# The first projection, the rotation tables and their place in the load queue

## The chip, the cores and the metric

The kernel runs on one core of one Trainium2 chip. Its engines are PE (TensorE, the matmul engine), DVE (VectorE), ACT (ScalarE), POOL (GpSimd) and SP (SyncE, which here only issues loads). They run their own instruction lists in order and wait for each other on semaphores. The metric is the device time of one execution in microseconds; less is better.

## The reference, cut to what matters

Two transformer-like blocks are computed on 256 tokens of width 1024. Only the front of the first one is touched here:

```
cs  = silu(c);  mod = cs @ mod_w[0] + mod_b[0]        # 1024 -> 6144: shift, scale, gate ...
h   = modulate(rms_norm(x, norm_g[0,0]), sh1, sc1)
proj = h @ ab_w_in                                     # 1024 -> 2048: u, q, k, v of 512 each
ab  = exp(lam * dt)                                    # complex, 32 groups x 64 states
x_t = ab * x_(t-1) + (b @ u_t);  y_t = Re(c @ x_t) + d_skip * u_t
y_ssm = gelu(y) * sigmoid(gelu(y) @ glu_w + glu_b)
y_att = attention of 8 heads of 64 with a bias per distance
x  += g1 * (concat(y_ssm, y_att) @ ab_w_out)
```

All data are float32.

## The kernel before, in words

**Weights and splits.** A stream of weight chunks, 128 x 2048 floats (1 MB) each, is loaded by SP into three buffers `raw[0..2]` (`load`, L573). ACT copies a chunk to `w_hi` in the type fp32r (`hi`, L745, the copy L751), DVE computes `w_lo = raw - w_hi` (`lo`, L1335, L1339). A product is then three fp32r matmuls, hi*hi, hi*lo and lo*hi (`three`, L2232). The activations are split in the same way into `h_hi` and `h_lo`. A `raw` buffer is free for the next chunk as soon as both halves have been made, long before PE uses them.

**The front.** PE computes the first 2048 modulation values from 16 pieces of 512 KB (`pm_piece`, L2183, four matmuls a piece, one for each 32 columns of the array), of which eight are in flight: six in `arena` and two in `raw[2]`. ACT takes the sums off (`pm_copy`, L881), PE turns them to columns (L2190), DVE adds the bias and makes the gains (L1493, L1524). x is normalized by DVE (L1517), turned by PE (`x_turn`, L2106), modulated by ACT (`x_upper`, L793, L795) and split by DVE (`x_lower`, L1540, L1541). The first chunk of `ab_in` is asked for behind twelve pieces.

**The projection `ab_in`** has 8 chunks of 16 products each (8 slices of the inner size, 2 output halves). Behind chunk c stand on PE `bu(c+1)` (input of state tile c+1, L2287) and, from c = 2, `y_of(c-2)` (output of a state tile, L2300). ACT copies a chunk out of PSUM (L905) and makes `w_hi` of chunk c+3; DVE makes `w_lo` of chunk c+3 and then runs `ssm_tile(c)` (L1611): multiply by the rotation table (L1615, L1616), add (L1618, L1619), scan (L1621), rotate back (L1630, L1632).

**The rotation tables** `e_re`, `e_im` hold cos and sin of angle * t for 16 tiles and 256 steps. They are outer products of two tables of 16 entries, made two tiles at a time by `e_pair` (L491, six operations L497 to L502): four pairs on DVE, four on POOL.

**The eight heads** follow. For head h, DVE runs `ssm_tile(8+h)`, `recip(h-1)` (L1667), `head(h)` (bias and maximum, L1658, L1661) and `turned_back(8+h)` (L1641, L1642). ACT scales the probabilities of head h-1 (`probs`, L913), takes the exponential of head h (L933), copies the turned probabilities of h-1 (L919) and last the output of h-1 (`head_copy`, L924). PE runs `bu`, `y_of`, the turn of head h-1 (L2106), up to five more modulation pieces, `head_out(h-1)` (L2352) and `scores(h+1)` (L2332). `y_out(n)` (L1647, DVE) adds the skip term to four finished tiles. Then come gelu (L944), the gate (`glu`, one chunk) and `ab_out` (four chunks).

Of the kernel before, what the change touches and what calls it, by code (L numbers as in the profile page):

```python
# [25 lines left out]
P = 128  # L26
T = 256
# [12 lines left out]
UT = SSM_G * SSM_H // P  # L40
HEADS, HD = 8, 64
# [33 lines left out]
CM_GROUPS = (2, 0, 3, 1)  # L75

# [179 lines left out]
def build(nc, A, out):  # L256
    with ExitStack() as ctx:
# [56 lines left out]
        e_re, e_im = at(E_TABLE, ST, T), at(E_TABLE + ST * T, ST, T)  # L314
# [4 lines left out]
        e1, e2 = (at(PREP + 512 * i, 2, ST, 16) for i in range(2))  # L319
        e_part = [at(a, 2, 16, 16) for a in (PREP + 1024, ARENA - 512)]  # L320
# [10 lines left out]
        pm_w = [at(a, PM_COLS) for a in (0, 1024, 2048, 3072, E_TABLE + 1024, E_TABLE + ST * T + 1024)]  # L331
        pm_w += [raw[2][:, i * PM_COLS:(i + 1) * PM_COLS] for i in range(2)]
        pm_late = [raw[i // 2][:, i % 2 * PM_COLS:(i % 2 + 1) * PM_COLS] for i in range(PM_LATE)]
        c_raw = hf[:, 0:4, :].rearrange("p (e a) (b c) -> p e (a b) c", e=2, c=32)
        c_tmp = [hf[:, 4 + 2 * i:6 + 2 * i, :].rearrange("p a (b c) -> p (a b) c", c=32) for i in range(2)]
# [153 lines left out]
        E_POOL = ST // 4  # L489

        def e_pair(v, link, g):  # L491

            j = slice(2 * g, 2 * g + 2)
            a, b = ([e[:, i, j, :].unsqueeze(k).broadcast_to([P, 2, 16, 16]) for i in range(2)] for e, k in ((e1, 3), (e2, 2)))
            er, ei = (t[:, j, :].rearrange("p j (a b) -> p j a b", b=16) for t in (e_re, e_im))
            part = e_part[g >= E_POOL]
            v.tensor_tensor(er, a[0], b[0], ALU.mult)  # L497
            link(v.tensor_tensor(part, a[1], b[1], ALU.mult))
            link(v.tensor_tensor(er, er, part, ALU.subtract))
            v.tensor_tensor(ei, a[0], b[1], ALU.mult)  # L500
            link(v.tensor_tensor(part, a[1], b[0], ALU.mult))
            return v.tensor_tensor(ei, ei, part, ALU.add)  # L502
# [49 lines left out]
        for n, v in enumerate(NORMS):  # L552
            pairs = v["kt"] // 2
            SQ.append(SQ[-1] + (0 if n in TOKEN or n == LAYER_NORM else pairs))
            UPPER.append(UPPER[-1] + (0 if n in (FINAL, FINAL_2) else DT // 2 if n in TURNED else 2 * pairs))
            SCALES.append(SCALES[-1] + (0 if n in TOKEN or n == LAYER_NORM else pairs))
            H.append(H[-1] + (pairs if n not in (FINAL, FINAL_2) else 0))

# [13 lines left out]
        def _(sp):  # L572
            def load(q, i=None):  # L573
# [60 lines left out]
            for m in range(PM_FIRST):  # L634
                load_pm(m)
                if m == 11:
                    load_plain("ab_in", 0, 1)
            load_plain("ab_in", 1, 2)
            sp.wait_ge(sem("pm_used"), PM_FIRST)
            load_plain("ab_in", 2, 6)  # L640
            sp.wait_ge(sem("h_ready"), H[1])
# [5 lines left out]
            sp.wait_ge(hi_done, Q["ab_out"] + 2)  # L647
            sp.wait_ge(lo_done, Q["ab_out"] + 2)
# [93 lines left out]
        def _(act):  # L742
            nxt = [0]

            def hi(q, i=None):  # L745
# [3 lines left out]
                if q >= SLOTS:  # L749
                    act.wait_ge(chunk_done, q - SLOTS + 1 + (0 if i is None else 6 * i))  # L750
# [33 lines left out]
            def x_upper(n):  # L784

                v, i = NORMS[n], TURNED.index(n)
                if n == 0:
                    act.wait_ge(sem("gates_known"), 1)
# [75 lines left out]
            act.dma_start(c_raw, A["ssm_c"].rearrange("p (e j c) -> p e j c", e=2, j=ST)).then_inc(sem("c_landed"), 16)  # L864
            act.dma_start(b_turned, A["ssm_b"].rearrange("p (e t s) -> p e t s", e=2, t=UT)).then_inc(sem("b_landed"), 16)
# [23 lines left out]
            hi_upto(0)  # L889
            pm_copy(1)  # L890
            x_upper(0)
            hi_upto(2)

            for c in range(8):
# [432 lines left out]
        def _(dve):  # L1327
# [92 lines left out]
            nc.vector.tensor_tensor(n0, abi, lr, ALU.mult)  # L1420
            link(nc.vector.tensor_tensor(n1, abr, li, ALU.mult))
            link(nc.vector.tensor_tensor(ci, n0, n1, ALU.subtract))
            link(nc.vector.tensor_tensor(ci, ci, den, ALU.mult))

            final_g = par[:, COL["final_g"]:COL["final_g"] + DT]
            nc.vector.tensor_tensor(both_g[:], final_g, par[:, COL["norm_mix_g_2"]:COL["norm_mix_g_2"] + DT], ALU.mult)
            link(nc.vector.tensor_tensor(both_q, final_g, final_g, ALU.mult))
            nc.vector.tensor_scalar(both_q, both_q, EPS, None, ALU.add).then_inc(sem("both_sum"), 1)
            dve.wait_ge(sem("c_landed"), 16)
# [1360 lines left out]
```

## Time and profile before

| | |
|---|---|
| median of 3 runs | 1525.33 us |
| lowest, highest | 1524.75, 1529.95 us |
| profiled execution, span from first to last instruction | 1526.8 us |
| PE, PEld, DVE, ACT, POOL busy | 94%, 78%, 74%, 51%, 3% |
| mean granted TensorE clock | 0.979 of full |
| chunk 0 of `ab_in` done (its copy L905 starts) | 64.84 us |
| chunk 7 done | 127.88 us |
| last head copied out | 200.84 us |

No time of the profiled execution is given beside its span; the span is 1.5 us above the median of the runs. An fp32 matmul stands in the profile as two instructions, an fp32r matmul as one. A row of the timeline gives a start in us, a duration in us, the engine, line, operation, tiles and shapes, and in brackets how long the engine had been idle and what ended that. A row of the chain gives start, duration and what it was.

### The profile page before, as it was taken

The numbers are of one execution on the slowest core, as the hardware profiler recorded it, in microseconds if no ns is written. First come the engines' busy times: TensorE is split into PE (matmuls) and PEld (weight loads), VectorE is DVE, ScalarE is ACT, GpSimd is POOL, SyncE is SP. The second block draws the span as 40 slices with busy tenths as digits, with TensorE's granted clock in tenths as the row PEclk, the third lists the DMA queues.
The fourth block names the chain that finished last, engine by engine and source line by source line (L and its number), as shares of the span: only waits on it lengthen the run. The fifth ranks groups of instructions, "written<-read, shape, count | busy, mean of one in ns | idle before, by whom it ended". The sixth has DMA issues, their size and how long they took to land.

```text
span 1526.8 us, 24920 instructions
## 1 busy us (share of the span) xinstructions
PE 1429.8 (94%) x9483; PEld 1193.0 (78%) x9483; DVE 1128.1 (74%) x1680; ACT 772.9 (51%) x1090; POOL 51.5 (3%) x38
## 2 busy tenths in 40 slices
PE   5498989999999999999999889999999999999998
PEld 1385568899976668999979655799997877799997
DVE  7999746988884457999984476686667858776666
ACT  3322356555563365555554666564546542455554
POOL 2600200000000000000001000000000000000000
PEclk9898999999999999999999999999999999999999
DMA  9332945988869766988734401355545433345551
GB/s 359 134 129 90 347 162 197 354 318 306 313 242 390 303 230 252 353 342 334 287 147 138 125 0 48 115 186 192 192 170 191 162 111 138 111 169 189 185 196 59
DMA packets 58060, 315.65 MB, mean 207 GB/s; under 512 B 7011, under 2 KB 8524, under 8 KB 33856
## 3 DMA queue, kind: packets, MB, share of 16 engines
q1 hardware_dynamic: 53826, 303.30, 53.8%
q10 hardware_dynamic: 4158, 11.30, 2.3%
q8 instruction: 52, 0.85, 0.2%
q14 instruction: 24, 0.20, 0.0%
HBM read 311.85 MB, written 1.15 MB: 205 GB/s over the span
## 4 chain that ended last, share of the span: by engine, by line
PE 75%; DVE 13%; ACT 5%; issue 4%; DMA 2%; ACTq 0%; SPq 0%; DVEq 0%; POOL 0%
PE bank L2232 62%; DVE w_lo L1339 2%; PE bank L2491 2%; ACT w_hi L751 1%; PE bank L2575 1%; PE bank L2106 1%; PE bank L2124 1%; PE bank L2183 1%; DMA arena<-in_mod_later 1%; PE bank L2300 1%; ACT hf L1256 1%; DVE h_lo L1541 1%; DVE hf L1553 1%; ACT hf L793 1%; DVE hf L1993 1%
## 5 line engine op out<-in xcount | busy, mean ns | idle before, releaser
L1339 DVE TENSOR_TENSOR w_lo<-raw,w_hi 128x2048 fp32r<-128x2048 f32 x186 | 426.2, 2292 | 169.6 <-ACT w_hi L751 168.4
L2232 PE MATMUL bank<-h_hi,w_hi 128*128 128x256 f32 x1800 | 517.3, 287 | 11.3 <-DVE h_lo L1541 9.7
L2232 PE MATMUL bank<-h_lo,w_hi 128*128 128x256 f32 x1800 | 510.8, 284 | 0.0
L2232 PE MATMUL bank<-h_hi,w_lo 128*128 128x256 f32 x1800 | 510.7, 284 | 0.0
L751 ACT ACTIVATE w_hi<-raw 128x2048 fp32r<-128x2048 f32 x186 | 355.8, 1915 | 129.8 <-PE bank L2232 114.6
L2232 PEld LDWEIGHTS bank<-h_hi,w_hi 128*128 128x128 f32 x1800 | 347.1, 193 | 21.3 <-DVE h_lo L1541 11.9
L2232 PEld LDWEIGHTS bank<-h_lo,w_hi 128*128 128x128 f32 x1800 | 347.0, 193 | 2.3 <-issue 0.7
L2232 PEld LDWEIGHTS bank<-h_hi,w_lo 128*128 128x128 f32 x1800 | 346.7, 193 | 0.0
L1756 DVE SCALAR_TENSOR_TENSOR arena<-bank,par,arena 128x255 f32<-128x255 f32 (+1 forms) x264 | 109.1, 475 | 111.5 <-ACT arena L988 79.1
L2232 PE MATMUL bank<-w_hi,a_hi 128*128 128x512 f32 x368 | 145.8, 396 | 4.9 <-DVE a_lo L1781 4.0
L2232 PE MATMUL bank<-w_hi,a_lo 128*128 128x512 f32 x368 | 144.3, 392 | 0.0
L2232 PE MATMUL bank<-w_lo,a_hi 128*128 128x512 f32 x368 | 144.1, 391 | 0.0
L988 ACT ACTIVATE arena<-bank,par 128x256 f32<-128x256 f32 x88 | 44.9, 560 | 139.4 <-PE bank L2232 139.4
L1367 DVE SCALAR_TENSOR_TENSOR arena<-arena,silu_c 128x384 f32<-128x384 f32 (+1 forms) x192 | 104.2, 611 | 0.0
L2232 PE MATMUL bank<-w_hi,h_hi 128*128 128x512 f32 (+1 forms) x224 | 86.5, 386 | 5.8 <-DVE hf L1553 3.0
L2232 PEld LDWEIGHTS bank<-w_hi,a_hi 128*128 128x128 f32 x368 | 69.6, 189 | 22.1 <-DVE w_lo L1339 5.0
L2232 PE MATMUL bank<-w_hi,h_lo 128*128 128x512 f32 (+1 forms) x224 | 84.8, 378 | 0.0
L2232 PE MATMUL bank<-w_lo,h_hi 128*128 128x512 f32 (+1 forms) x224 | 84.7, 378 | 0.0
L2232 PEld LDWEIGHTS bank<-w_lo,a_hi 128*128 128x128 f32 x368 | 69.5, 189 | 15.0
L2232 PEld LDWEIGHTS bank<-w_hi,a_lo 128*128 128x128 f32 x368 | 69.6, 189 | 13.0
L1006 ACT ACTIVATE a_hi<-arena 128x512 fp32r<-128x512 f32 x44 | 27.8, 632 | 61.9 <-DVE arena L1777 61.8
L2232 PEld LDWEIGHTS bank<-w_hi,h_hi 128*128 128x128 f32 x224 | 42.9, 191 | 18.4 <-issue 10.7
(327 smaller groups left out, 1703.5 us busy)
## 6 DMA issues: line engine op xcount, KB each, us to landing
raw<-in_stream SPq DMA_DIRECT2D x186, 1024.0 KB, 5.0
arena<-in_mod_stream SPq DMA_DIRECT2D x64, 768.0 KB, 7.5
arena<-in_mod_later SPq DMA_DIRECT2D x48, 512.0 KB, 8.0
raw<-in_mod_pe SPq DMA_DIRECT2D x36, 512.0 KB, 6.6
arena<-in_mod_pe SPq DMA_DIRECT2D x12, 512.0 KB, 12.7
sq<-row_store ACTq DMA_DIRECT2D x7, 512.0 KB, 3.5
sq<-in_bias SPq DMA_DIRECT2D x8, 256.0 KB, 6.7
x<-in_x_t ACTq DMA_DIRECT2D x1, 1024.0 KB, 8.6
```

The lines of the kernel that those rows point to most:

```text
L751: nc.scalar.activation(w_hi[s][:], raw[s][:], ACT.Copy).then_inc(hi_done, 1)
L793: nc.scalar.activation(hf[:, k, :], turned(n, k), ACT.Identity, **by).then_inc(sem("full_ready"), 1)
L988: ins = nc.scalar.activation(gate_c[:, e, :], half(4, e), ACT.Identity, scale=par[:, bass.ds(wb[center] + 2 * s + e, 1)], bias=par[:, bass ...
L1006: nc.scalar.activation(slot_hi(q), act_f, ACT.Copy)\
L1256: nc.scalar.activation(mla_s(h, t), bank[u % 4][:], ACT.Exp, bias=small[:, k + 1:k + 2], scale=MLA_SCALE, accum_out=small[:, k + 2:k + 3]) ...
L1339: nc.vector.tensor_tensor(w_lo[s][:], raw[s][:], w_hi[s][:].bitcast(F32), ALU.subtract).then_inc(lo_done, 1)
L1367: ins = nc.vector.scalar_tensor_tensor(parts[e], buf[:, kt % 4, :], silu_c[:, c0 + kt:c0 + kt + 1], parts[e], ALU.mult, ALU.add)
L1541: ins = nc.vector.tensor_tensor(v["parts"][1][:, k, :], hf[:, k, :], up.bitcast(F32), ALU.subtract)
L1553: ins = nc.vector.tensor_tensor(part, acc[:], row_at(gate_rows[gate], fh), ALU.mult)
L1756: ins = nc.vector.scalar_tensor_tensor(o, src, par[:, bass.ds(w[tap] + 2 * s + e, 1)], o, ALU.mult, ALU.add)
L2232: ins = nc.tensor.matmul(out_, l, r, start=first and n == 0, stop=last and n == 2, **kw)
L2491: ins = nc.tensor.matmul(bank[2 * part + ft][:], dft[:, part, t, ft * P:(ft + 1) * P], sources[part][:, t, 512 * s_:512 * s_ + 512], start ...
```

## The change

1. The eight `ab_in` chunks are not split (PLAIN = 8). PE multiplies `raw` by the unsplit `hf` in fp32 (`plain_chunk`), 16 matmuls a chunk in place of 48. The hi/lo counters start at chunk 8. A `raw` buffer is now free when PE has finished the chunk in it (`chunk_done`), up to chunk 10.
2. The normalized input is modulated once, four slices by ACT and four by DVE, with no `h_hi`, `h_lo`.
3. The tables are doubled instead: DVE makes 64 steps of all tiles in six rounds, and the steps to 128 and to 256 come tile by tile, each from two ACT copies with a scale (`twist`) and one DVE operation (`double`). POOL makes no tables.
4. The skip term is a PE matmul with a diagonal (`skip_diag`) that opens the sum of four tiles; `y_out` becomes an ACT copy.
5. Loads: the pieces use four buffers in `arena` and four in `raw[1]`, `raw[2]`; the first `ab_in` chunk is asked for behind all sixteen pieces; `ssm_b` and `ssm_c` move from ACT's queue at the start to SP's queue behind it; `x_turn(0)` stands behind piece 12 instead of 15; x is scaled before the tables are made, and the C matrix is prepared after the modulation.

```
-                if q >= SLOTS:
-                    sp.wait_ge(hi_done, q - SLOTS + 1 + more)
-                    sp.wait_ge(lo_done, q - SLOTS + 1 + more)
+                if q >= SLOTS + PLAIN:
+                    sp.wait_ge(hi_done, q - SLOTS + 1 - PLAIN + more)
+                    sp.wait_ge(lo_done, q - SLOTS + 1 - PLAIN + more)
+                elif q >= SLOTS:
+                    sp.wait_ge(chunk_done, q - SLOTS + 1)
...
-                if m == 11:
+                if m == 15:
                     load_plain("ab_in", 0, 1)
+            sp.dma_start(b_turned, A["ssm_b"]...)
+            sp.wait_ge(sem("pm_used"), 14)
             load_plain("ab_in", 1, 2)
+            sp.dma_start(c_raw, A["ssm_c"]...)
             sp.wait_ge(sem("pm_used"), PM_FIRST)
             load_plain("ab_in", 2, 6)
...
+            def twist(j, m):                                          # ACT
+                i = doubling(j, m)
+                if i == 1:
+                    act.wait_ge(sem("doubled"), 1)
+                if m == 2 * BASE:
+                    act.wait_ge(sem("doubled"), 1 + doubling(j, BASE))
+                k = m // BASE - 1
+                nc.scalar.activation(turns_[:, j, 0, m:2 * m], turns_[:, j, 1, 0:m], ACT.Copy, scale=pow_neg[:, k, j:j + 1])
+                nc.scalar.activation(turns_[:, j, 1, m:2 * m], turns_[:, j, 0, 0:m], ACT.Copy, scale=pows[6 + k][:, 1, j:j + 1])\
+                    .then_inc(sem("twisted"), 1)
...
             for c in range(8):                                        # ACT
                 nc.scalar.activation(dst, src, ACT.Copy).then_inc(bank_free, 1)
                 hi_upto(q + 3)
+                twist(c + 4, BASE)
+                twist(c + 2, 2 * BASE)
+                if c == 6:
+                    y_out(0)
...
             for h in range(HEADS):                                    # ACT
+                if h < 4:
+                    twist(12 + h, BASE)
+                if h < 6:
+                    twist(10 + h, 2 * BASE)
...
+            def double(j, m):                                         # DVE
+                k = m // BASE - 1
+                dve.wait_ge(sem("twisted"), doubling(j, m))
+                nc.vector.scalar_tensor_tensor(turns_[:, j, :, m:2 * m], turns_[:, j, :, 0:m], pows[6 + k][:, 0, j:j + 1],
+                                               turns_[:, j, :, m:2 * m], ALU.mult, ALU.add).then_inc(sem("doubled"), 1)
...
             for c in range(8):                                        # DVE
                 lo_upto(Q["ab_in"] + c + 3)
+                double(c + 4, BASE)
                 ssm_tile(c)
-                if c in (2, 4):
-                    link(e_pair(nc.vector, link, 1 + c // 2))
+                double(c + 2, 2 * BASE)
             for h in range(HEADS):
-                if h % 2 == 0:
-                    dve.wait_ge(sem("e_ready"), h // 2 + 1)
+                if h < 4:
+                    double(12 + h, BASE)
                 ssm_tile(8 + h)
+                if h < 6:
+                    double(10 + h, 2 * BASE)
...
+            def plain_chunk(c, q, fill):                              # PE
+                w = raw[q % SLOTS]
+                pe.wait_ge(raw_landed[q % SLOTS], LANDED[q])
...
+                    ins = nc.tensor.matmul(half(4 + fill % 2, n), *sides, start=c > 0 and k == 0, stop=k == DT - 1, skip_group_check=c == 0)
+                ins.then_inc(chunk_done, 1)
```

ACT, from the output copy of head 0 (L924 before, L944 now) to that of head 1. L913/L933 scale, L933/L961 exponentiate, L919/L939 copy the turned probabilities, L881/L872 is `pm_copy`. Before:

```order
L924 ACTIVATE arena<-bank 64x256
L913 ACTIVATE hf<-hf,small 128x256 x2
L933 ACTIVATE hf,small<-hf,small 128x256 x2
L919 ACTIVATE hf<-bank 128x512
L881 ACTIVATE arena<-bank 128x256
L924 ACTIVATE arena<-bank 64x256
```

Now:

```order
L944 ACTIVATE arena<-bank 64x256
L884 ACTIVATE arena<-arena 128x64
L885 ACTIVATE arena<-arena 128x64
L884 ACTIVATE arena<-arena 128x128
L885 ACTIVATE arena<-arena 128x128
L933 ACTIVATE hf<-hf,small 128x256 x2
L961 ACTIVATE hf,small<-hf,small 128x256 x2
L939 ACTIVATE hf<-bank 128x512
L872 ACTIVATE arena<-bank 128x256
L944 ACTIVATE arena<-bank 64x256
```

The first two of the four copies between them are `twist(14, 64)`, the other two `twist(12, 128)`.

DVE, from `turned_back(9)` (L1682, L1683) on, over tile 10 (L1656 to L1671), `recip(1)` (L1702) and `head(2)` (L1693, L1696), with the two `double` operations (L1625). Before, the same operations have the lines L1641 and L1642, L1615 to L1630, L1667 and L1658:

```order
L1641 TENSOR_TENSOR arena<-arena 128x256
L1642 TENSOR_TENSOR arena<-arena 128x256
L1615 TENSOR_TENSOR arena<-bank,arena 128x512
L1616 TENSOR_TENSOR arena<-bank,arena 128x512
L1618 TENSOR_TENSOR arena<-arena 128x256
L1619 TENSOR_TENSOR arena<-arena 128x256
L1621 SCALAR_TENSOR_TENSOR arena<-cols,arena 128x256 x2
L1630 TENSOR_TENSOR arena<-arena 128x512
L1667 RECIPROCAL small<-small 128x2
L1658 SCALAR_TENSOR_TENSOR hf<-bank,sq 128x512
```

Now:

```order
L1682 TENSOR_TENSOR arena<-arena 128x256
L1683 TENSOR_TENSOR arena<-arena 128x256
L1625 SCALAR_TENSOR_TENSOR arena<-arena 128x2x64
L1656 TENSOR_TENSOR arena<-bank,arena 128x512
L1657 TENSOR_TENSOR arena<-bank,arena 128x512
L1659 TENSOR_TENSOR arena<-arena 128x256
L1660 TENSOR_TENSOR arena<-arena 128x256
L1662 SCALAR_TENSOR_TENSOR arena<-cols,arena 128x256 x2
L1671 TENSOR_TENSOR arena<-arena 128x512
L1625 SCALAR_TENSOR_TENSOR arena<-arena 128x2x128
L1702 RECIPROCAL small<-small 128x2
L1693 SCALAR_TENSOR_TENSOR hf<-bank,sq 128x512
```

Added are `double(14, 64)` ahead of tile 10 and `double(12, 128)` behind it, each of which waits for its `twist`.

## Rows read from the trace of the kernel before

**Rows 1.** PE timeline, last modulation piece and x_turn (start us, us, what)
```profile
34.30 1.04 PE L2183 MATMUL bank<-raw,arena 128*32 128x256 f32 x8 [0.20 <-DMA raw<-in_mod_pe]
...
35.27 1.97 PE L2106 MATMUL bank<-ident_sb,hf 128*128 128x128 f32 x16
```

**Rows 2.** Windows (us; PE, PEld, DVE, ACT, POOL busy; PEclk; DMA share, GB/s)
```profile
6.00:33.00 27.00, 16.09 (x116) 3.78 (x116) 22.74 (x104) 10.86 (x23) 3.25 (x3) 1.00 1.02 412
...
76.00:80.00 4.00, 4.00 (x20) 3.86 (x20) 3.93 (x5) 0.00 (x0) 0.00 (x0) 0.57 0.48 203
...
144.00:154.00 10.00, 7.68 (x49) 3.34 (x50) 9.73 (x19) 2.83 (x9) 2.28 (x2) 0.52 0.33 115
```

**Rows 3.** DVE groups from 29.7 to 64 us (count, busy us, mean ns)
```profile
L1541 DVE TENSOR_TENSOR h_lo<-hf,h_hi 128x256 fp32r<-128x256 f32 x8 | 10.3, 1322 | 0.1
```

**Rows 4.** DVE groups from 64 to 135 us, same columns
```profile
L1339 DVE TENSOR_TENSOR w_lo<-raw,w_hi 128x2048 fp32r<-128x2048 f32 x10 | 22.8, 2289 | 1.7 <-ACT w_hi L751 1.5
...
L1618 DVE TENSOR_TENSOR arena<-arena 128x256 f32<-128x256 f32 x8 | 3.4, 425 | 0.3
```

**Rows 5.** DVE timeline: column arithmetic, powers, last table round (start us, us, what)
```profile
11.26 0.18 DVE L1409 TENSOR_TENSOR cols<-cols 128x16 f32<-128x16 f32 x1 [0.30 <-ACT cols L875]
...
14.33 0.68 DVE L1432 TENSOR_TENSOR hf<-hf,cols 128x512 f32<-128x512 f32 x1
...
18.77 0.17 DVE L1440 COPY arena<-cols 128x16 f32<-128x16 f32 x1
...
22.33 0.21 DVE L1458 TENSOR_TENSOR arena<-arena 128x32 f32<-128x32 f32 x1
...
28.30 0.43 DVE L1458 TENSOR_TENSOR arena<-arena 128x256 f32<-128x256 f32 x1
```

**Rows 6.** Chain of waits, 75 to 93 us (start us, us, what)
```profile
75.11 1.10 PE bank L2287 x4
...
76.21 7.43 PE bank L2232 x48
...
84.70 1.84 PE bank L2300 x8
...
86.55 5.94 PE bank L2232 x48
```

**Rows 7.** Chain of waits near 1294 us, plain fp32 matmuls
```profile
1294.36 7.16 PE bank L2768 x32
```

**Rows 8.** ACT timeline after chunks 0 and 7 of ab_in
```profile
64.84 0.60 ACT L905 ACTIVATE arena<-bank 128x512 f32<-128x512 f32 x1 [7.43 <-PE bank L2232]
...
127.88 0.60 ACT L905 ACTIVATE arena<-bank 128x512 f32<-128x512 f32 x1 [6.44 <-PE bank L2232]
...
128.38 1.90 ACT L751 ACTIVATE w_hi<-raw 128x2048 fp32r<-128x2048 f32 x1
```

**Rows 9.** DMA issues, 73 to 107 us (count, KB, us to landing)
```profile
raw<-in_stream SPq DMA_DIRECT2D x5, 1024.0 KB, 4.8
```

**Rows 10.** DVE timeline, starts of tiles 7 and 9, and recip(0)
```profile
132.52 0.68 DVE L1615 TENSOR_TENSOR arena<-bank,arena 128x512 f32<-128x512 f32 x1
...
143.80 0.68 DVE L1615 TENSOR_TENSOR arena<-bank,arena 128x512 f32<-128x512 f32 x1
...
147.95 0.17 DVE L1667 RECIPROCAL small<-small 128x2 f32<-128x2 f32 x1
```

**Rows 11.** ACT timeline, exponential of head 0; head copies 0, 1, 2, 6
```profile
143.25 0.51 ACT L933 ACTIVATE hf<-hf,small 128x256 f32<-128x256 f32 x1 [11.67 <-DVE small L1661]
...
155.71 0.38 ACT L924 ACTIVATE arena<-bank 64x256 f32<-64x256 f32 x1 [4.65 <-PE bank L2352]
...
163.94 0.38 ACT L924 ACTIVATE arena<-bank 64x256 f32<-64x256 f32 x1 [2.71 <-PE bank L2352]
...
170.92 0.38 ACT L924 ACTIVATE arena<-bank 64x256 f32<-64x256 f32 x1 [2.71 <-PE bank L2352]
...
200.84 0.38 ACT L924 ACTIVATE arena<-bank 64x256 f32<-64x256 f32 x1 [0.89 <-PE bank L2352]
```

More of the change, by code:

```diff
@@ L75 @@
 CM_GROUPS = (2, 0, 3, 1)
+PLAIN = 8
 def consts():
@@ L488, in build, with doubling @@
         Y_BANK = (2, 6, 2, 5)
[L489 to L502, printed above, removed]
+        DOUBLED = [(j, BASE) for j in range(4)] + [(j, 2 * BASE) for j in range(2)]
+        for _c in range(8):
+            DOUBLED += [(_c + 4, BASE), (_c + 2, 2 * BASE)]
+        for _h in range(6):
+            DOUBLED += [(_h + 12, BASE)] * (_h < 4) + [(_h + 10, 2 * BASE)]
+        def doubling(j, m):
+            return DOUBLED.index((j, m)) + 1
         FILL, _f = {}, 0
@@ L885, in _, with y_out @@
                 x_square(0, j, BY_TOKENS)
-            pm_copy(0)
+            def twist(j, m):
[8 more added lines that the diff above has]
+                    .then_inc(sem("twisted"), 1)
+            pm_copy(0)
+            for j in range(4):
+                twist(j, BASE)
+            pm_copy(1)
+            act.wait_ge(sem("gates_known"), 1)
+            for k in (0, 1, 4, 5):
+                if k % 4 == 0:
+                    act.wait_ge(sem("x_turned"), 3 + k // 4)
+                nc.scalar.activation(hf[:, k, :], turned(0, k), ACT.Identity, scale=gains[:, 0, k:k + 1], bias=mod[:, 0, k:k + 1])\
+                    .then_inc(sem("full_ready"), 1)
+            for j in range(2):
+                twist(j, 2 * BASE)
             act.wait_ge(sem("both_sum"), 1)
             nc.scalar.activation(both_q, both_q, ACT.Sqrt).then_inc(sem("both_q_ready"), 1)
[L889 to L892, printed above, removed]
+            def y_out(n):
+                act.wait_ge(sem("ssm_y_done"), 4 * n + 4)
+                nc.scalar.activation(u_t[:, n, :], half(Y_BANK[n], 0), ACT.Copy).then_inc(sem("y_ready"), 1)
             for c in range(8):
@@ L1425, in _ @@
[L1425 to L1429, printed above, removed]
-            crb, cib = (v.unsqueeze(2).broadcast_to([P, ST, 32]) for v in (cr, ci))
-            c_of = [c_turned[:, e].rearrange("p a (b c) -> p (a b) c", c=32) for e in range(3)]
@@ L1605, in _ @@
+            def double(j, m):
[3 more added lines that the diff above has]
+                                               turns_[:, j, :, m:2 * m], ALU.mult, ALU.add).then_inc(sem("doubled"), 1)
+            for j in range(4):
+                double(j, BASE)
             first_mod_out(0, 2)
             x_gains(0)
-            x_lower(0)
@@ L1608, in _ @@
-            lo_upto(2)
-            link(e_pair(nc.vector, link, 1))
+            for k in (2, 3, 6, 7):
+                if k % 4 == 2:
+                    dve.wait_ge(sem("x_turned"), 3 + k // 4)
+                nc.vector.tensor_scalar(hf[:, k, :], turned(0, k), gains[:, 0, k:k + 1], mod[:, 0, k:k + 1], ALU.mult, ALU.add)\
+                    .then_inc(sem("h_ready"), 1)
+            for j in range(2):
+                double(j, 2 * BASE)
+            dve.wait_ge(sem("c_landed"), 16)
+            crb, cib = (v.unsqueeze(2).broadcast_to([P, ST, 32]) for v in (cr, ci))
@@ L2292, in y_of @@
                 n, r = j // 4, 32 * (j % 4)
-                if j % 4 == 0 and n >= 2:
-                    pe.wait_ge(sem("y_ready"), n - 1)
+                if j == 0:
+                    pe.wait_ge(sem("c_ready"), 1)
+                if j % 4 == 0:
+                    if n >= 2:
+                        pe.wait_ge(sem("y_ready"), n - 1)
+                    nc.tensor.matmul(half(Y_BANK[n], 0), skip_diag[:, n, :], u_t[:, n, :], start=True, stop=False, skip_group_check=True)
                 c_, s_ = by_cos[j % 2], by_sin[j % 2]
```

220 lines of the change are left out of this document (110 added, 110 removed).

## The prediction

> **What bounds the kernel now.** The page first: PE is busy for 94% of the span and holds most of the chain, so outside the front nothing that the change touches can matter. The front is read by windows, by the chain of waits and engine by engine, with the question when chunk 0 of `ab_in` is done, when chunk 7 is, and when the last head is. ACT begins to copy chunk 0 at 64.84 us and chunk 7 at 127.88 [rows 8]; the heads follow, and all behind them comes in one piece.
>
> Up to 64.8 us PE is not the bound. The last piece starts at 34.30 and ends at 35.3 [rows 1], and from then on DVE makes tables and splits. While POOL makes its tables, a subtraction of 256 elements takes DVE 1.32 us [rows 3], against 0.425 for one of that size afterwards [rows 4]. From 75 to 128 us PE is the bound: a chunk is 5.94, `bu` 1.10, `y_of` 1.84 [rows 6], together 8.84 a chunk. In the heads it is a ring of all three engines.
>
> **1. To the end of chunk 0.** From 6 to 33 us the DMA engines move 412 GB/s, saturated [rows 2]. Ahead of the last piece stand today C and B (0.5 MB each) and chunk 0 (1 MB): 2.1 MB, or 5.1 us. The last piece lands at about 29 us in place of 34.2. PE then lags: `x_turn(0)` (1.97 us [rows 1], perhaps double) now stands between pieces 12 and 13, and three pieces of 1.04 follow, so piece 15 ends at 31.5 to 33.5. ACT's copy, PE's turn, DVE's bias and gains and the first modulated slices take about 2.3 more. Chunk 0 lands some 2.5 us behind piece 15, in time.
>
> DVE must be ready by then. Its column arithmetic is 3.1 us (11.26 to 14.33), the powers 3.6 (18.77 to 22.33) [rows 5]. Rounds of the table grow from 0.7 us at 32 elements; the 256-element round at 28.30 takes 1.3 [rows 5], so 512 and 1024 are 2.1 and 3.7, and six rounds 9.4. With the scaling of x (2.3), the diagonal and four doublings (1.7) this ends at 31.7. That is close, but not last.
>
> A chunk in fp32 is 16 matmuls, 32 instructions. The same shape and count near 1294 us took 7.16 us [rows 7]. Chunk 0 is done at 34.5 + 7.2, about 42 (41 to 46). Term: 42.0 - 64.8 = **-22.8**.
>
> **2. Chunks 1 to 7.** Before, 127.88 - 64.84 = 63.0. Now the first two take 0.6 + 1.1 + 7.16 = 8.8 each, the other five 7.16 + 1.06 + 1.84 = 10.06 each, plus two diagonal matmuls of 0.45 (two of the 32 instructions in rows 7) and about 0.7 for a wait (step 3): 69.5. Splitting on DVE (2.29 a chunk [rows 4]) and ACT goes away, but lay beside PE. What also goes is a wait ahead of chunk 2 and its slow start (7.43 for 5.94 [rows 6]), which is in the 63.0. Term: **+6.5**.
>
> **3. Loads behind the projection.** A `raw` buffer used to come free when split; now when PE is through. Chunks 8, 9 and 10, still split, are therefore asked for only when chunks 5, 6 and 7 are done. In front of tiles 5, 6 and 7, DVE waits for the load, ACT's half and its own half. Landing takes 4.8 us [rows 9], `w_hi` 1.90 [rows 8], `w_lo` 2.2, a doubling 0.3: tile 7 starts 9.3 us behind chunk 7. Today it is 132.52 - 127.88 = 4.6 [rows 8, 10]. For tiles 5 and 6 PE has ten us of other work as cover (0.7 short once). Term: **+4.7**.
>
> **4. Doublings in DVE's chain.** From tile 7 to `recip(0)` DVE is never idle today. It gains two doublings of 64 steps (128 elements, 0.25) and three of 128 (256 elements, near the 0.425 of rows 4, 0.37 when overlapped), and loses `y_out(1)`, 0.4. `double(13, 64)` stands in front of tile 9, which starts 0.5 us after the exponential of head 0 [rows 10, 11]; its `twist` is behind that exponential (1.1 us) on ACT, so it waits 0.9. Term: 0.5 + 1.1 - 0.4 + 0.9 = **+2.1**.
>
> **5. A ring in heads 2 and 3.** `twist(14, 64)` stands on ACT behind `head_copy(0)`, and `double(14, 64)` in front of tile 10 on DVE; heads 3 and tile 11 are alike. Today tile 10 does not wait for that copy. Now everything is in series: head copy 0.4, twist 0.5, doubling 0.3, tile 4.15 (143.80 to 147.95 [rows 10]), second doubling 0.4, then from `recip` to the next head copy what today is 155.71 - 147.95 = 7.8 [rows 10, 11], less 2.1 because the pieces in it ran at half clock (a window at 0.52 [rows 2]): 5.7. Sum 11.4 a head. Today the copies are 8.23 and 6.98 apart [rows 11]. Term: 22.8 - 15.2 = **+7.6**. From head 4 on no doubling stands in front of a tile, and I add nothing.
>
> The unknown price is the twist: ACT instructions of 64 and 128 elements with a scale from a tile. Lower bound 0.2 for the pair (a pair hidden in the gaps of other work), upper 1.0 (twice the 0.51 of a 256-element ACT instruction [rows 11]). I take 0.5, as the fixed part weighs most. The Trainium skill, ScalarE: Activation LUTs, What ACT_TABLE_LOAD costs, gives 186 ns + 0.833 ns an element, 93 more for each pointer operand and 93 of overlap. By that page's figures the pair of 64 elements would be an estimated 0.48.
>
> **6. The end.** `y_out(3)` on ACT waits for the last `y_of` in front of gelu, whose table load starts at once today: **+1.0**.
>
> **7. Clock.** Behind the wait that ends at 75.11 PE's granted clock was at its half level, 1.2 GHz: the window from 76 shows 0.57 [rows 2], and a chunk took 7.43 for 5.94 [rows 6]. Steps 3 and 5 make waits of 7, 3.5 and 3.5 us. In heads 2 and 3 I count one burst of pieces in two at half rate: **+2.1** (0 to 4.2).
>
> Sum: -22.8 + 6.5 + 4.7 + 2.1 + 7.6 + 1.0 + 2.1 = +1.2. Against the profiled execution's span of 1526.8 that is 1528.0; the median of the runs is 1.5 lower, 1525.33, so 1526.5, rounded to **1527**.
>
> **Rivals.**
> *The ring does not close.* If PE, with its up to five pieces a head, stays the bound and the late tiles lie beside it, step 5 and half of step 7 fall away: -7.6 - 1.1, 1518; with chunk 0 at 41 it is 1517. For it: PE is busy 7.68 of 10 us from 144 on even while it waits for probabilities [rows 2], and a tile has had slack there. Against: the order of ACT and DVE puts the tile strictly behind the copy, and PE's next turn behind the tile. The front arriving whole (-16) would need step 3 to vanish too: 1509.
>
> *Slower: PE starts cold each time.* The place is chunk 0 and the pieces of heads 2 and 3. Pieces up to 35 us took 1.04 us [rows 1], while five took 2.29 at 168 us [rows 6]; they ran at the pace of the half level, whatever the window's granted clock of 1.00 says. If chunk 0 runs at half rate for half of its length, +3.6; if both bursts are cold, +2.1 more; if `x_turn` is cold too, +1.5. That is 1534. It decides when chunk 0 ends behind 45 us. The Trainium skill, TensorE: Matmul & The Clock Gate, HAM oscillation, says that bursts shorter than the waits between them are throttled anew and start cold every time. The trace agrees once, in the 7.43 of rows 6. By that rule every burst behind the waits of steps 3 and 5 is at half rate, which is this rival.
>
> *The front is later for another reason:* DVE's strided table rounds take longer than I scaled them. Two us more and DVE is last; six more give 1533.
>
> **Chances.** Forecast 0.62, spread 1521 to 1532; ring open 0.13; whole gain 0.03; cold starts 0.15; late tables 0.07. About 0.5% (7.6 us) is what a measurement of this kernel can tell from no change. Faster by more takes the open ring below 1517.7 and the whole gain: 0.14. Slower by more, above 1533, takes most of the last two: 0.19. Within: 0.67. The range that leaves two in ten is 1516 to 1535.
>
> **What would show it.** Copy of chunk 0 at 41 to 46 us; chunks 10.1 us apart; copy of chunk 7 at 111 to 115; tile 7 some 9 us behind it; a wait of ACT for `raw` of 4 to 5 us in front of `w_hi`; head copies 0 to 3 about 11 us apart; DVE waiting 4 to 6 us for ACT's twist in front of tiles 10 and 11; last head copy at 197 to 204. I am wrong if tiles 10 and 11 start without a wait, if the chunks are not 10 us apart, or if chunk 0 ends behind 46.

## The result and the profile after

The changed kernel takes 1535.89 us (median of five, 1535.15 to 1542.53) against 1529.95 for the kernel before on the same chip: a ratio of 1.0051, 95% interval 1.0034 to 1.0067. It is slower by half a per cent. The forecast, 1527 against 1525.33, was a ratio of 1.0011. The profiled execution has a span of 1533.3 us against 1526.8, 6.5 more, so the two profiles can be laid side by side to see where this comes from.

ACT's timeline after (start us, us, what, idle time before) answers to [rows 8, 11]: the copies of chunks 0 and 7, the last half of a split, head copies 0, 1, 2 and 6, and the gelu table.

```profile
41.31 0.60 ACT L921 ACTIVATE arena<-bank 128x512 f32<-128x512 f32 x1 [4.65 <-PE bank L2356]
...
111.07 0.60 ACT L921 ACTIVATE arena<-bank 128x512 f32<-128x512 f32 x1 [3.20 <-PE bank L2356]
116.19 1.91 ACT L746 ACTIVATE w_hi<-raw 128x2048 fp32r<-128x2048 f32 x1 [4.53 <-DMA raw<-in_stream]
...
147.80 0.38 ACT L944 ACTIVATE arena<-bank 64x256 f32<-64x256 f32 x1 [4.54 <-PE bank L2397]
...
162.64 0.38 ACT L944 ACTIVATE arena<-bank 64x256 f32<-64x256 f32 x1 [2.82 <-PE bank L2397]
...
176.05 0.38 ACT L944 ACTIVATE arena<-bank 64x256 f32<-64x256 f32 x1 [3.46 <-PE bank L2397]
...
206.73 0.38 ACT L944 ACTIVATE arena<-bank 64x256 f32<-64x256 f32 x1 [0.89 <-PE bank L2397]
...
208.12 1.28 ACT L973 ACT_TABLE_LOAD   x1
```

Chunk 0 comes 23.5 us sooner (64.84 before). By chunk 7 the lead is 16.8. ACT then waits 4.53 us for a load, and head copy 0 is only 7.9 ahead. Head copy 2 is already 5.1 *behind* (170.92 before): the two gaps are 14.84 and 13.41 where they were 8.23 and 6.98. The gelu table is loaded at 208.12 against 201.23. So 6.7 of the 23.5 us are spent in chunks 1 to 7, and the other 16.8, with 5.1 more, between chunk 7 and head copy 2.

A plain chunk in the chain of waits (start us, us, what), to be held against the 5.94 of [rows 6]:

```profile
43.20 7.12 PE bank L2356 x32
```

The chain of waits after, through one head, from head copy 0 to head copy 1:

```profile
147.80 0.38 ACT arena L944
148.17 0.24 ACT arena L884
148.41 0.25 ACT arena L885
148.69 0.03 DVE arena L1625
...
148.96 0.68 DVE arena L1656
...
153.10 0.07 DVE arena L1625
153.16 1.22 issue
154.39 0.16 DVE small L1702
154.57 0.92 ACT hf L933 x2
...
155.53 1.12 PE bank L2136 x4
156.65 2.76 PE bank L2213 x24
159.44 0.39 ACT arena L872
...
159.87 0.72 PE bank L2220 x4
160.60 1.00 PE bank L2213 x16
161.60 1.02 PE bank L2397 x4
162.64 0.38 ACT arena L944
```

This is the ring: head copy, twist (L884, L885), doubling (L1625), tile (L1656), second doubling, `recip` (L1702), probabilities (L933), turn (L2136), pieces (L2213) with a copy and a turn between them (L872, L2220), `head_out` (L2397), head copy. Nothing else is on it. Two prices stick out: 1.22 us of "issue" behind the second doubling's first 0.07 (together most of that doubling's 1.36), and PE's 1.12 for a turn that takes 0.59 elsewhere. The chain of before, in the same head, is PE's but for one copy of ACT between the pieces. Its turn and its first three pieces take about half as long; its last two take the same 1.00:

```profile
158.76 0.59 PE bank L2106 x4
159.35 1.48 PE bank L2183 x24
...
161.89 1.00 PE bank L2183 x16
```

DVE's timeline after, around the first doubling of a head:

```profile
129.44 0.69 DVE L1671 TENSOR_TENSOR arena<-arena 128x512 f32<-128x512 f32 x1
130.17 1.36 DVE L1625 SCALAR_TENSOR_TENSOR arena<-arena 128x256 f32<-128x256 f32 x1
```

and POOL's:

```profile
129.49 1.76 POOL L728 TENSOR_TENSOR arena<-arena 128x512 f32<-128x512 f32 x1 [129.03 <-DVE arena L1662]
```

The doubling ends 0.3 us behind POOL's instruction. All four doublings of 256 elements in heads 0 to 3 take 1.36 or 1.37, and each ends 0.27 to 0.30 us behind POOL's; with POOL silent they take 0.48 or 0.49.

Windows after (us; PE, PEld, DVE, ACT, POOL busy; PEclk; DMA), answering to the third row of [rows 2]:

```profile
141.00:148.00 7.00, 6.66 (x49) 3.25 (x50) 1.32 (x3) 2.06 (x7) 0.00 (x0) 0.61 0.51 153
148.00:155.00 7.00, 2.85 (x12) 1.39 (x10) 6.18 (x11) 1.66 (x7) 1.77 (x1) 0.88 0.68 261
155.00:163.00 8.00, 6.96 (x54) 3.67 (x55) 1.48 (x4) 2.79 (x9) 0.00 (x0) 0.68 0.53 169
```

PE and DVE work in turns, seven to eight microseconds each. PE begins each burst at its half level and is back at the full one by its end: the last two pieces and `head_out` take 1.00 and 1.02 in the chain above, as before.

### The profile page after: what moved, and what is told of

It is laid out like the page before. It is cut to its first block, busy times and chain, and to the rows that moved or that the text cites. A ratio compares the mean times of both kernels' runs of the same rounds, so it can differ in the third digit from the quotient of the medians.

```text
span 1533.3 us, 24753 instructions
## 1 busy us (share of the span) xinstructions
PE 1441.6 (94%) x9349; PEld 1196.7 (78%) x9363; DVE 1089.6 (71%) x1664; ACT 773.2 (50%) x1142; POOL 19.6 (1%) x14
## 4 chain that ended last, share of the span: by engine, by line
PE 76%; DVE 9%; ACT 5%; issue 5%; DMA 4%; SPq 0%; ACTq 0%; DVEq 0%; POOL 0%
PE bank L2263 60%; PE bank L2356 3%; PE bank L2536 2%; PE bank L2136 2%; ACT w_hi L746 1%; DMA raw<-in_stream 1%; PE bank L2213 1%; DMA arena<-in_mod_pe 1%; DVE w_lo L1368 1%; PE bank L2620 1%; PE bank L2154 1%; DMA arena<-in_mod_later 1%; DVE hf L1524 1%; ACT hf L786 1%; DVE arena L1396 1%
## 5 line engine op out<-in xcount | busy, mean ns | idle before, releaser
L2263 PE MATMUL bank<-h_hi,w_hi 128*128 128x256 f32 x1704 | 487.2, 286 | 2.2 <-ACT arena L1229 0.9
L2263 PE MATMUL bank<-h_lo,w_hi 128*128 128x256 f32 x1704 | 482.0, 283 | 0.0
L2263 PE MATMUL bank<-h_hi,w_lo 128*128 128x256 f32 x1704 | 482.0, 283 | 0.0
L2263 PEld LDWEIGHTS bank<-h_hi,w_hi 128*128 128x128 f32 x1704 | 326.8, 192 | 9.2 <-issue 4.1
L2263 PEld LDWEIGHTS bank<-h_lo,w_hi 128*128 128x128 f32 x1704 | 326.7, 192 | 2.3 <-issue 0.7
L2263 PE MATMUL bank<-w_hi,h_hi 128*128 128x512 f32 x192 | 76.9, 401 | 5.8 <-DVE hf L1524 3.0
L2263 PE MATMUL bank<-w_lo,h_hi 128*128 128x512 f32 x192 | 75.3, 392 | 0.0
L2263 PE MATMUL bank<-w_hi,h_lo 128*128 128x512 f32 x192 | 75.3, 392 | 0.0
L2136 PEld LDWEIGHTS bank<-ident_sb,hf 128*128 128x128 f32 x304 | 38.9, 156 | 36.6 <-ACT hf L933 15.8
L2136 PE MATMUL bank<-ident_sb,hf 128*128 128x128 f32 x304 | 47.2, 303 | 19.6 <-ACT hf L933 13.1
```

The lines of the kernel that those rows point to most:

```text
L2136: return nc.tensor.transpose(out_, in_, ident[0:n, 0:n])
L2263: ins = nc.tensor.matmul(out_, l, r, start=first and n == 0, stop=last and n == 2, **kw)
```

## Experiments

The yardstick is the time from the copy of chunk 0 to the gelu table load, read on ACT's timeline; it leaves out a front that differs by up to 3 us from one profile to the next (chunk 0 was copied between 40.8 and 43.8 us in kernels whose fronts are the same; chunk 0's own multiplications took 7.17 us in most of them, but 8.86 in e2 and e12 and 9.73 in e9). Before: 136.4. After: 166.8. Ratios are to the kernel before.

| kernel | ratio (95%) | copy 0 to gelu | tile 7 to recip(0) | gaps of head copies |
|---|---|---|---|---|
| changed, again | 1.0050 (1.0029, 1.0071) | 166.6 | 19.6 | 14.8, 13.4 |
| e1, doubling later on DVE | 0.9999 (0.9981, 1.0017) | 162.9 | 17.0 | 15.5, 12.2 |
| e2, twists sooner on ACT | 0.9969 (0.9953, 0.9986) | 155.0 | 19.6 | 8.8, 7.7 |
| e12, both | 0.9917 (0.9900, 0.9934) | 150.9 | 17.0 | 8.2, 7.5 |
| e3, all in the chunk loop | 0.9922 (0.9900, 0.9944) | 149.2 | 15.0 | 8.2, 7.1 |
| e4, splits a chunk later | 1.0028 (1.0010, 1.0046) | 165.9 | 20.7 | 16.6, 14.4 |
| e6, e3 and e4 | 0.9889 (0.9859, 0.9919) | 146.5 | 17.2 | 8.2, 7.0 |
| e7, PE kept busy | 1.0016 (0.9995, 1.0036) | 163.4 | 19.6 | 14.6, 11.9 |
| e11, for longer | 1.0013 (0.9996, 1.0029) | 161.6 | 19.6 | 13.0, 11.9 |
| e5, old order of loads | 1.0050 (1.0030, 1.0070) | 168.6 | 19.6 | 16.6, 14.4 |
| e9, e6 and two more | 0.9902 (0.9883, 0.9921) | 143.8 | 17.2 | 8.3, 7.1 |

### The ring: e2

```
                 ins.then_inc(sem("exp_ready"), 1)
+                twists(h + 1)
                 if h:
                     probs_copy(h - 1)
```

`twists(h)` holds the two twists that stood at the start of head h.

> Against the changed kernel. ScalarE makes the two twists of head h+1 right behind exp(h), ahead of probs_copy(h-1) and head_copy(h-1); VectorE's order is unchanged. Theory A (the ring head_copy, twist, doubling, tile, scores, exp, probs, turn, head_copy sets the gaps between head copies): VectorE's waits of 6.4 and 7.2 us for the twist at 148.7 and 163.7 vanish, the gaps of 14.84 and 13.41 fall to 9 to 11 each: -7 to -9 us, 1527 to 1529. Rival C (the gaps are long since TensorE runs at a granted 0.55 to 0.78 there and the late pieces and turns take longer): the waits move to another place and the gaps stay over 12.5: 1532 to 1536.

The gaps fell by 6.0 and 5.8. One call moved in ACT's order takes the changed kernel from 0.5% slower to 0.3% faster. The gaps are now 8.8 and 7.7, shorter than the 9 to 11 expected. Rival C, a slow PE as the cause, falls: with the ring open, the turn of head 1 is at its full rate by itself, and so is all behind it. PE in e2:

```profile
152.13 0.66 PE L2140 MATMUL bank<-ident_sb,hf 128*128 128x128 f32 x4
152.72 1.50 PE L2217 MATMUL bank<-raw,arena 128*32 128x256 f32 x24
```

From head 1 on the low level was a consequence of the ring. The turn and pieces of head 0 are still slow in e2 (1.11 and 3.82 us).

### The doubling beside GpSimd: e1, and both orders: e12

```
                 ssm_tile(8 + h)
-                if h < 6:
-                    double(10 + h, 2 * BASE)
 ...
                 if h < HEADS - 1:
                     turned_back(8 + h)
+                if h < 6:
+                    double(10 + h, 2 * BASE)
```

> Against the changed kernel (1535.9). On VectorE the doubling of tile 10+h (128 columns) is moved from behind tile 8+h, where it runs beside GpSimd's multiplication and takes 1.36 us, to behind turned_back(8+h), when GpSimd has ended. Theory A (a VectorE doubling is held until GpSimd's instruction ends, about 0.9 us each in heads 0 to 3, all of it in the chain tile, recip, head copy): each doubling takes 0.49 in its new place, most of it in idle time; tile 7 to recip(0) falls from 19.6 to about 18.2, the first two gaps between head copies by about 1.4 each from 14.84 and 13.41: 1532, -4 us. Rival B (the doubling takes 1.36 for a reason of its own, such as ScalarE's twist just before it): it still takes over 1.2 us and is merely late next: gaps fall by under 0.5 each, 1535.

On DVE and on POOL of e1:

```profile
131.72 0.48 DVE L1625 SCALAR_TENSOR_TENSOR arena<-arena 128x256 f32<-128x256 f32 x1
```

```profile
129.05 1.77 POOL L728 TENSOR_TENSOR arena<-arena 128x512 f32<-128x512 f32 x1 [128.59 <-DVE arena L1662]
```

The same instruction takes 0.48 when POOL has ended, in heads 0, 1 and 2 alike; rival B falls. A tile in front of `recip` is 4.15 long again, for 5.43. With the twists still on the ring not all of it comes through: tile 7 to `recip(0)` gave 2.6, but the gaps together only 0.6, since head 1 took 10.2 us from `recip` to the head copy instead of 8.3, all of it PE's at the lower level. The profiles are 4.2 us apart; the ratio moved by 0.5%, which with both intervals is 4 to 12 us.

> Both edits of order together, e2_ring (twists of head h+1 ahead of probs_copy(h-1)) and e1_behind (doubling of tile 10+h behind turned_back): no work moved to the chunk loop. Theory: e2 stands at 0.9969 with VectorE as the bound of heads 0 to 3 (its doublings beside GpSimd still take 1.37); e1's edit gives 1.3 us in each of four tiles on top: gaps near 8.2 and 7.0, tile 7 to recip(0) 17.0, -4 us, 0.994. Rival: the doubling behind turned_back now stands in VectorE's queue ahead of the next tile with no idle time to cover it, and takes 0.5 to 0.9 of the 1.3 back: 0.9955 or more.

With both orders the gaps are nearly those of before (8.23 and 7.50 us against 8.23 and 6.98), and nothing had to be moved to another stage. The theory holds; its rival does not.

### No doubling in the heads: e3

```
+        for _c in range(7):
+            DOUBLED += [(2 * _c + 4 + e, BASE) for e in range(2) if _c < 6] + [(2 * _c + 2 + e, 2 * BASE) for e in range(2)]
```

and the calls of `twist` and `double` in the chunk loop follow this list; those in the heads go.

> Against the changed kernel. All twists and doublings are made in the chunk loop (two of 64 and two of 128 columns behind each chunk), none is left for the heads. Theory A (ring and doublings beside GpSimd cost the heads their time): the first two gaps come back to the 8.2 and 7.0 of before, tile 7 to recip(0) to 15.4, at no more than 2 us in the chunk loop, which TensorE paces: -13 -4 +1 = -16, 1520. Rival C (low clock set by the front): gaps stay over 11, 1528 or more. Rival D (ScalarE and VectorE have no room left in the chunk loop: 1.1 and 1.0 us more a chunk): chunks 5 to 7 take over 10.5 each and the gain is under 10.

Tile 7 to `recip(0)` and the first two gaps come back, at no cost in the chunk loop: chunk 7 was copied 70.0 us behind chunk 0, 69.8 in the changed kernel. Rivals C and D fall. Head copies 2 to 6 lie 31.6 us apart for 29.9 before; that was not looked into. Head copies of e3:

```profile
141.96 0.38 ACT L944 ACTIVATE arena<-bank 64x256 f32<-64x256 f32 x1 [3.44 <-PE bank L2393]
...
150.20 0.38 ACT L944 ACTIVATE arena<-bank 64x256 f32<-64x256 f32 x1 [2.71 <-PE bank L2393]
...
157.30 0.38 ACT L944 ACTIVATE arena<-bank 64x256 f32<-64x256 f32 x1 [2.83 <-PE bank L2393]
```

and its window, to be held against 0.88 and 2.85 above:

```profile
148.00:155.00 7.00, 7.00 (x62) 3.85 (x65) 4.93 (x11) 2.98 (x8) 1.77 (x1) 1.00 1.00 367
```

### The loads of chunks 8 to 10: e4 and e6

```
-                hi_upto(q + 3)
+                hi_upto(q + 2)
 ...
-                lo_upto(Q["ab_in"] + c + 3)
+                lo_upto(Q["ab_in"] + c + 2)
```

Chunk 10 is split by ACT behind the chunk loop and by DVE in head 0.

> Against the changed kernel. The splits of chunks 8 and 9 come one chunk later on ScalarE and VectorE, that of chunk 10 in head 0, so that no engine waits for a load that was asked for only when its slot came free (4.1, 4.1 and 4.5 us of waiting of ScalarE at 94.6, 104.6 and 116.2). Theory A (the step of the loads, +4.7 predicted and +4.9 measured): tile 7 starts 4.5 to 6 us behind the copy of chunk 7 instead of 9.5; the new place of chunk 10's split falls in idle time: -4 to -5 us, 1531. Rival E (tile 7 is late since VectorE's own queue is full there): it moves by under 2 us, or what it gains is waited away at recip(0): over 1534.

> Against e3_early (0.9922 of before, 1518.6): its early doublings, and the splits of chunks 8 to 10 one chunk later as in e4_splits. Theory A: tile 7 starts 4 to 5 us sooner behind chunk 7, and since no head waits for a twist any more nothing gives that back: -4 to -5, 0.989 to 0.990 of before, 1514. Rival F (what e4 showed: of 4.0 us won at recip(0), 2.8 were lost again between the head copies, since TensorE at its lower level has longer pieces to make there): -1 to -2, 1517.

Tile 7 starts 4.9 and 4.6 us behind the copy of chunk 7 instead of 9.5, so the step of the loads is as it was told. What it is worth depends on the ring. In time e4 is not clear of the changed kernel (1.0028 and 1.0051, with overlapping intervals). In e4 `recip(0)` came 4.0 sooner against chunk 0 and head copies 1 and 2 gave 2.8 of it back: PE's pieces and `head_out` took longer at the lower level. In e6, with the ring open, the yardstick is 2.7 shorter than in e3, between the two expectations. Tile 7 started 5.4 us sooner against chunk 0. DVE's half of chunk 10's split, which now stands between tiles 8 and 9, took 2.2 of that, and the burst from `recip(0)` to head copy 0 another 1.4 (7.9 us for 6.6, its pieces 4.50 for 3.31). The ratios of e3 and e6 overlap, so that in time the step from one to the other is not shown.

### PE kept busy: e7 and e11

```
+                if 1 <= h <= 3:
+                    for _ in range(20):
+                        nc.tensor.matmul(half(5, 0), zeros[:, 0:P], zeros[:, 0:T], start=True, stop=True)
                 if h:
                     head_turn(h - 1)
```

> Against the changed kernel: TensorE multiplies 20 times 256 columns of zeros into an unused bank ahead of the turns of heads 0, 1 and 2, while it waits for the ring (idle 2.7, 4.7 and 4.8 us there). Theory C2 (the slow pace of TensorE behind these waits is a part of the ring's size: turn 1.12 for 0.59, five pieces 3.4 to 4.3 for 2.3): the granted clock stays at 1.00 from the second head on, the turn takes 0.6, the pieces 1.9 to 2.3, the gaps 14.84 and 13.41 fall by 1.5 to 2.5 each, 4 to 6 us in all: 1530 to 1532. Rival G (the pieces wait for their loads, or the dummies run past the ring and delay the turn): the gaps move by under 0.7, 1535 or more.

> Against e7_awake (1.0016 of before): 40 instead of 20 multiplications of zeros ahead of the turns of heads 1 and 2, since 20 ended 2.4 us before the turns at 152.8 and 167.5, and head 1's turn still took 1.12 and its pieces 3.6. Theory C2: with the idle time filled, head 1's turn takes 0.6 and its pieces 2.3: the gap of 14.60 falls to about 12.8, that of 11.87 stays: -1.5 to -2, 1.0004. Rival G: the dummies end behind the moment at which the turn could start and delay it: gaps 0 to 1 us longer.

e11 makes 20 such multiplications ahead of head 0's turn, as e7 does, and 40 ahead of those of heads 1 and 2. PE in e7 in front of the turns of heads 1 and 2:

```profile
148.02 2.36 PE L2411 MATMUL bank<-zeros 128*128 128x256 bf16 x20
152.77 1.12 PE L2136 MATMUL bank<-ident_sb,hf 128*128 128x128 f32 x4 [2.39 <-ACT hf L933]
...
167.51 0.66 PE L2136 MATMUL bank<-ident_sb,hf 128*128 128x128 f32 x4 [2.53 <-ACT hf L933]
```

and in e11 in front of head 1's:

```profile
148.37 4.54 PE L2411 MATMUL bank<-zeros 128*128 128x256 bf16 x40
153.12 0.66 PE L2136 MATMUL bank<-ident_sb,hf 128*128 128x128 f32 x4 [0.21 <-ACT hf L933]
153.71 1.50 PE L2213 MATMUL bank<-raw,arena 128*32 128x256 f32 x24
```

After 2.39 us of idleness the turn ran at half the pace (1.2 GHz), after 0.21 us at the full one. In head 2 of e7 it was at the full one after a wait of 2.53 us too. Ahead of both waits PE had worked at the full rate, so neither the wait nor the pace before it decides alone, and what does is open here. That also is why e7's expectation missed the first gap, which moved by 0.24 us instead of 1.5 to 2.5; the second moved by 1.54, and the burst of head 0 shrank by 2.5. From `recip` to the head copy heads 0, 1 and 2 take 7.6, 8.3 and 6.7 us in the changed kernel and 5.1, 6.4 and 5.2 in e11: the low level costs 5.9 us in the three. Rival G falls: the 40 multiplications end ahead of the turns and delay none. In time e7 brought about 5 us (1.0016 for 1.0050; by the two intervals 1 to 10), 3.4 on the yardstick; e11's further 1.8 us of the yardstick do not show in its ratio. The Trainium skill, TensorE: Matmul & The Clock Gate, HAM oscillation, says that bursts shorter than the waits between them are throttled anew each time. Here PE works for 9.5 us (141.34 to 150.85) and waits for 4.68 in the changed kernel, and the turn behind is slow all the same; so the trace agrees that a burst behind a wait can start slow, but bursts longer than the waits, for which the prediction used this rule, are not what the page speaks of.

### The order that the change is named for: e5 and e10

Both change one number: e5 puts chunk 0's load back behind piece 11 in the changed kernel, e10 puts it behind piece 15 in the kernel before.

> Against the changed kernel: chunk 0 of ab_in is asked for behind piece 11 again, not behind piece 15; all else as changed. Theory (step 1 of the prediction, the loads of the front run at 412 GB/s): pieces 12 to 15 land 1 MB or 2.5 us later, VectorE's doublings end at 32.1 and no longer cover anything, so the copy of chunk 0 moves from 41.3 to about 43.7 and all behind it by the same: +2.4 us. Rival (TensorE's slow pieces and x_turn, or VectorE's tables, set the front and not the loads): the copy of chunk 0 moves by under 1 us.

> The kernel before with only the one edit that the change's name tells of: chunk 0 of ab_in asked for behind piece 15, not 11. Theory (VectorE's tables and splits beside GpSimd set the front of before from 35 to 65 us, not the loads): the last piece ends at 33 instead of 35.3, the copy of chunk 0 stays within 1 us of 64.8, and the time is 1.000 of before. Rival (the loads set it): the copy comes 2.5 us sooner, 0.9985.

In e10 the last piece started 2.7 us sooner (31.61 for the 34.30 of [rows 1]), and chunk 0 was copied when it always was (64.84 before, [rows 8]):

```profile
31.61 0.97 PE L2183 MATMUL bank<-raw,arena 128*32 128x256 f32 x8 [0.21 <-DMA raw<-in_mod_pe]
```

```profile
65.05 0.60 ACT L905 ACTIVATE arena<-bank 128x512 f32<-128x512 f32 x1 [7.42 <-PE bank L2232]
```

The ratio is 0.9995 (0.9979, 1.0011): nothing, as the theory had it. In e5 chunk 0 was copied at 42.15 against 41.31 and 40.79 in two profiles of the changed kernel: 0.8 to 1.4 us, not 2.4. PE waits 1.75 us for piece 12 and starts it 1.29 us later. What follows is slow work of PE's own in either kernel, a piece at 1.08 us and an `x_turn` (3.22 here, 3.68 there), and the pieces behind have landed by the time it comes to them:

```profile
27.10 1.08 PE L2213 MATMUL bank<-raw,arena 128*32 128x256 f32 x8 [1.75 <-DMA raw<-in_mod_pe]
28.11 3.22 PE L2136 MATMUL bank<-ident_sb,hf 128*128 128x128 f32 x16
```

By this one profile the order of the loads is worth about a microsecond, between the theory's 2.4 and the rival's "under 1". That is no more than the profiles of like fronts differ by, and the ratio (1.0050, as the changed kernel's) shows nothing of it, so its size is not shown. In e5 22.7 of the 23.5 us are there, so they come from the rest of the front.

### The best version: e8 and e9

e8 is the changed kernel again. Its first two gaps agree with the first profile to 0.03 us.

> The changed kernel itself once more, as the common measure for the runs beside it: 1.0051 of before within 0.0015, with gaps of 14.8 and 13.4 us between the first three head copies. If the gaps in a second profile differ by over 1 us, single profiles of the heads can't be compared to better than that.

> e6_both (0.9889 of before, 1513.6) with two more edits: 20 multiplications of zeros ahead of the turn of head 0 alone (that burst took 7.9 us from recip(0) to the head copy in e6, 5.1 in e7 where TensorE was kept busy), and y_out(3) behind the first gelu, so that the load of the gelu table does not wait for the last y_of. Theory: -2.7 and -1.0: from recip(0) to head copy 0 5.2 us, last head copy to first gelu 0.4 instead of 1.4, 1510, 0.9865 of before. Rival: the time won in head 0 is waited away at the next turn, since VectorE's tiles then set the pace; under -1.5, 1512 or more.

The yardstick of e9 is 2.7 shorter than that of e6, the table load follows the last head copy by 0.4 us, as expected, and `recip(0)` to head copy 0 takes 6.4 instead of 7.9, not 5.2: the fifth piece of that burst now landed too late, 6.8 us behind its request, and that request waits for the split of chunk 10.

```profile
131.47 6.84 DMA raw<-in_mod_pe
```

In time it is no better than e6: 0.9902 (0.9883, 0.9921), for an expected 0.9865, where its profile had a front 1.7 us later. Both beat the two kernels of this case, by 1.0 to 1.1% the one before.

## Why the prediction was wrong

Its own terms, on the two profiles:

| step | predicted | measured |
|---|---|---|
| 1, end of chunk 0 | -22.8 | -23.5 |
| 2, chunks 1 to 7 | +6.5 | +6.7 |
| 3, loads behind the projection | +4.7 | +4.9 |
| 4, tile 7 to `recip(0)` | +2.1 | +4.15 |
| from there to head copy 0 | 0 | -0.15 |
| 5 and 7, head copies 0 to 2, and the clock | +9.7 | +13.0 |
| head copies 2 to 6 | 0 | +0.8 |
| 6, to gelu | +1.0 | +1.0 |
| sum | +1.2 | +6.9 |

Steps 1, 2, 3 and 6 held, with their mechanisms: e4 shows the third, e9 the sixth. The ring of step 5 is there, exactly between the instructions that the prediction named, and e2 opens it. What failed are sizes in steps 4, 5 and 7.

**Doublings, steps 4 and 5.** The prediction took "0.37 when overlapped" for a doubling of 256 elements, from the 0.425 of [rows 4]. Two of them stand between tile 7 and `recip(0)` beside POOL and cost 0.9 more each (1.29 and 1.28 us to the next start, for the 0.37), nearly all of the 2.05 that step 4 missed; one in each turn of the ring makes the tile up to `recip` 5.43 and 5.44 instead of 4.55. e1 shows the cause. The row that gave it away was used in the prediction for another purpose: 1322 ns for an instruction with two inputs of 256 elements beside POOL's tables [rows 3]. That GpSimd works in the heads too stood in the third row of [rows 2] (2.28 us in two instructions), and the price was not carried over. The Trainium skill, SBUF — State Buffer, SBUF: two separate sides, has the rule: VectorE with two inputs from SBUF and a GpSimd instruction that reads SBUF exclude each other, and the later one waits for the whole of the other. The trace agrees on three instructions: the doubling, begun inside POOL's 1.76 us, is held; the multiplication at 129.44, 0.05 us ahead of POOL, takes its ordinary 0.69; and the scores' instruction, one of whose inputs is in PSUM, takes 0.69 right inside POOL's time in e1.

**From `recip` to the head copy, steps 5 and 7.** Step 5 took 5.7 at full rate and step 7 added 2.1 for both heads. At full rate it is 6.4 and 5.15 (e11): head 1 holds a copy of piece sums and their turn, which the prediction left out. The low level adds 1.9 and 1.5, as the burst starts slow in both heads and not in one of the two. Together 14.9 for the 13.5 of the sum.

With step 4's 2.05 and the 1.8 of the doublings in the ring that is 5.3 of the 5.7 that the sum is short. The rival "PE starts cold each time" forecast 1534 and is nearest in number, but only a part of its mechanism: the bursts of the heads and `x_turn` (3.68 us) were slow, chunk 0 was not (7.19 us). That it was not is partly luck of the profile: the same 32 instructions took 8.86 us in e2 and e12 and 9.73 in e9. "The ring does not close" fell outright.

Two of the signs that the prediction named tell the same: the head copies were to be 11 us apart and were 14.84 and 13.41, and DVE was to wait 4 to 6 us ahead of tiles 10 and 11 and waited 6.36 and 7.15. The 2.29 us that it gives for five pieces at 168 us is right, but stands in no group of rows; it is this line of the chain before:

```profile
167.58 2.29 PE bank L2183 x40
```

The last part of the miss is no step: the kernel before took 1529.95 in the comparison and 1525.33 when the prediction was made, and the forecast in us carries that with it.

## What to carry to other kernels

When work is spread into another engine's slack, follow the order of each engine around once for every stage: a producer placed behind a consumer of the same round closes a ring, and the stage then costs the sum of three engines instead of the longest. Here two moved calls were worth 1.3% (1.0051 to 0.9917), more than the 0.5% that the change cost. Price an instruction with the neighbour that runs at its time, not by its size: here a VectorE doubling with two SBUF inputs took 1.36 us beside a GpSimd multiplication and 0.48 without it. A ring also makes TensorE wait, and here its bursts behind the waits started at the lower level, which cost 5.9 us in three heads.

## Not expected of the hardware

- From 22 to 31 us of the changed kernel the granted clock reads 1.00, yet a piece takes 1.08 us and the first `x_turn` 3.68, the pace of the half level; behind it three pieces take 1.50. In e12, whose front is the same, pieces and `x_turn` take as long in that window, and there it reads 0.50; e12's five pieces from 15 to 22 us took 0.64 or 0.65 each, under 0.99. The granted clock of a window did not tell the pace in the changed kernel's front. The window of the changed kernel, that of e12, and PE's timeline of the changed kernel:

```profile
22.00:31.00 9.00, 8.60 (x60) 5.22 (x60) 8.45 (x30) 2.02 (x8) 0.00 (x0) 1.00 1.01 404
```

```profile
22.00:31.00 9.00, 8.26 (x52) 5.17 (x56) 8.45 (x30) 2.02 (x8) 0.00 (x0) 0.50 1.01 407
```

```profile
23.85 1.08 PE L2213 MATMUL bank<-arena 128*32 128x256 f32 x8 [0.21 <-DMA arena<-in_mod_pe]
...
26.82 3.68 PE L2136 MATMUL bank<-ident_sb,hf 128*128 128x128 f32 x16
30.43 1.50 PE L2213 MATMUL bank<-raw,arena 128*32 128x256 f32 x24
```

- Two profiles of one kernel agree to 0.03 us in the gaps of a ring of three engines, but edits ahead of it (e4, e5) move them from 14.8 and 13.4 to 16.6 and 14.4, by slower work of PE (`head_out` 1.65 for 1.02 in e4). Why its level rises later there is open.
- Twist pairs on ScalarE with a scale from SBUF took 0.24 + 0.25 us at 64 columns in the chain: the 0.5 of the forecast.
